# A hybrid decoder step on one core: the second half of the third block's step table put into a new order

## The reference, cut to what matters

```python
qp, fp, ip, gp = _split(jnp.einsum('bld,de->ble', h, w_in), C_SPLITS)
f = lower_bound + (1.0 - lower_bound) * jax.nn.sigmoid(fp)
q, k, log_f, v = silu(qp), 1.0 - f, log(f), ip          # each in 8 heads
...
A = cumsum(log_f)                                        # in _hgrn2
s = einsum('bhtk,bhtsk->bhts', q, exp(A_t - A_s) * k)    # causal
o = q exp(A) S + s v;   S_new = exp(A_end) S + k exp(A_end - A) v
...
o = _head_norm(o, hg_gn, False) * silu(gp)
return einsum('ble,ed->bld', o, w_out), S_new
```

## Time and profile before

| | |
|---|---|
| median of 3 runs | 1481.58 us (1480.04 to 1482.13) |
| profiled execution, own time | 1482.85 us |
| its span, first to last instruction | 1481.0 us |
| TensorE busy | 1455.0 us, 98% of the span |
| VectorE, ScalarE busy | 78%, 63% |
| mean granted TensorE clock | 0.994 |

### The profile page before, as it was taken

The page is one execution under the profiler, slowest core; times in us unless marked ns, Lnnn a source line. Parts: engine busy times, 40 slices in busy tenths (PEclk is TensorE's granted clock), DMA queues, the critical chain, the costliest instruction groups (busy, mean ns, idle before and its releaser), DMA issues.

```text
span 1481.0 us, 23131 instructions
## 1 busy us (share of the span) xinstructions
PE 1455.0 (98%) x8514; PEld 1288.9 (87%) x8514; DVE 1148.0 (78%) x1283; ACT 936.2 (63%) x983; POOL 82.4 (6%) x97
## 2 busy tenths in 40 slices
PE   9999999999999989999999999999999999999997
PEld 8889889999999989888888888888888888888885
DVE  5766687554556697776888988989889888898997
ACT  5354755334334675363877878778787787877875
POOL 1023100000001000120300000000000000000011
PEclk9999999999999999999999999999999999999999
DMA  8578636996456523542999999999999999999994
GB/s 233 143 144 144 126 101 186 309 297 186 122 143 193 167 86 105 154 128 75 408 408 409 410 365 393 366 401 391 357 392 364 401 387 364 393 376 385 394 344 163
DMA packets 213733, 404.06 MB, mean 273 GB/s; under 512 B 13487, under 2 KB 130507, under 8 KB 213534
## 3 DMA queue, kind: packets, MB, share of 16 engines
q1 hardware_dynamic: 203120, 373.62, 72.2%
q0 software_dynamic: 6320, 22.21, 5.0%
q10 hardware_dynamic: 4222, 7.26, 1.3%
HBM read 372.76 MB, written 30.28 MB: 272 GB/s over the span
## 4 chain that ended last, share of the span: by engine, by line
PE 89%; DVE 6%; ACT 2%; issue 1%; DMA 1%; POOL 1%; SPq 0%; DVEq 0%; ACTq 0%; POOLq 0%
PE bank L536 26%; PE bank L538 26%; PE bank L537 26%; PE bank L1234 1%; PE bank L830 1%; PE bank L1048 1%; POOL expert_rows L2796 1%; DVE dense_lo L1982 1%; PE bank L793 1%; DMA ring<-in_w_in_ab 1%; PE bank L763 1%; DVE w_lo L2494 1%; PE bank L704 1%; ACT dense_hi L1462 1%; DMA expert_rows<-arena,IDX 0%
## 5 line engine op out<-in xcount | busy, mean ns | idle before, releaser
L2494 DVE TENSOR_TENSOR w_lo<-arena,w_hi 128x2048 fp32r<-128x2048 f32 (+1 forms) x280 | 596.7, 2166 | 76.3 <-ACT w_hi L1823 75.5
L1823 ACT ACTIVATE w_hi<-arena 128x2048 fp32r<-128x2048 f32 (+1 forms) x280 | 501.8, 1820 | 116.0 <-PE bank L538 105.2
L536 PE MATMUL bank<-w_hi,xg_hi 128*128 128x512 f32 x704 | 275.6, 391 | 0.5 <-DVE w_lo L2494 0.3
L538 PE MATMUL bank<-w_hi,xg_lo 128*128 128x512 f32 x704 | 274.1, 389 | 0.0
L537 PE MATMUL bank<-w_lo,xg_hi 128*128 128x512 f32 x704 | 274.0, 389 | 0.0
L1982 DVE TENSOR_TENSOR dense_lo<-ring,dense_hi 128x2048 fp32r<-128x2048 f32 (+1 forms) x77 | 165.6, 2150 | 127.6 <-ACT dense_hi L1462 127.6
L1462 ACT ACTIVATE dense_hi<-ring 128x2048 fp32r<-128x2048 f32 (+1 forms) x78 | 140.5, 1802 | 136.0 <-PE bank L538 110.5
L536 PEld LDWEIGHTS bank<-w_hi,xg_hi 128*128 128x128 f32 x704 | 132.2, 188 | 30.8 <-issue 3.1
L538 PEld LDWEIGHTS bank<-w_hi,xg_lo 128*128 128x128 f32 x704 | 132.1, 188 | 27.6
L537 PEld LDWEIGHTS bank<-w_lo,xg_hi 128*128 128x128 f32 x704 | 132.2, 188 | 26.9
L536 PE MATMUL bank<-h_hi,dense_hi 128*128 128x320 f32 x448 | 143.2, 320 | 3.3 <-DVE h_lo_a L2052 1.8
(11 more groups left out here) (474 smaller groups left out, 2333.0 us busy)
## 6 DMA issues: line engine op xcount, KB each, us to landing
arena<-in_w_moe_down SPq DMA_DIRECT2D x176, 512.0 KB, 6.8
arena<-in_w_moe_gate SPq DMA_DIRECT2D x128, 512.0 KB, 7.7
arena<-in_w_moe_up SPq DMA_DIRECT2D x128, 512.0 KB, 7.4
arena<-in_w_moe_gate SPq DMA_DIRECT2D x64, 384.0 KB, 4.2
arena<-in_w_moe_up SPq DMA_DIRECT2D x64, 384.0 KB, 5.2
ring<-in_w_in_ab SPq DMA_DIRECT2D x32, 512.0 KB, 8.7
ring<-in_w_in_c SPq DMA_DIRECT2D x32, 512.0 KB, 4.6
expert_rows<-ZERO SPq DMA_DIRECT2D x12, 1024.0 KB, 7.7
```

Source lines behind the costliest of these rows:

```text
L536: mm(out, left[0], right[0], start=start, stop=False)
L538: return mm(out, left[1], right[0], start=False, stop=stop)
L1823: fn(WH[SLOT_OF[p]][:, 0:unit_size(p)], STAGE[:, s, 0:unit_size(p)], ACT.Copy).then_inc(S("unit_hi"), 1)
L2494: v.tensor_tensor(WL[w][:, 0:n], STAGE[:, s, 0:n], WH[w][:, 0:n].bitcast(F32), ALU.subtract).then_inc(S("unit_split"), 1)
```

## The change

Six of the table's nine rows are replaced by five; the first three rows and the first nine steps of the fourth (`xend0` to `thin0`) stay. Two rows of before, two of after, and the edits of code:

```diff
-    lb2 db3 state0 turn1 v7 xb3 lb3 sq0 v8 thin2 wh pb3 out1 wl v9 turn2 db4 out2 thin3 sq1 db5 xb4 lb4 state1 v10 state2
-    pb4 db6 xb5 g0 lb5 turn3 sq2 xb6 wh v11 pb5 out3 wh wl pb6 sq3 lb6 wl g1 db7 xb7 g2 pb7 g3 lb7 end1 state3
...
+    xb3 lb3 v5 wh pb3 db4 lb4 xb4 v6 pb4 db5 state0 turn1 xb5 lb5 sq0 v7 thin2 pb5 db6 wl out1 xb6 lb6 v8 wh sq1 turn2 pb6 db7
+    out2 thin3 state1 xb7 lb7 v9 wl pb7 end1 lb8 xend1 v10 state2 sq2 turn3 v11 wh kend1 out3 g0 wl sq3 state3 turn4 thin4 turn5 thin5
...
@@ ScalarE, step silug
-                    if u == 2:
-                        nc.scalar.preload_act_table_set("sqrt_and_others")
@@ ScalarE, step h
+                    if u == KD - 1:
+                        nc.scalar.preload_act_table_set("sqrt_and_others")
@@ VectorE, step mixc
+                    if u == HEADS[1][0]:
+                        after_empty(dve, ("sp", 1, KD - 1))
```

More of the change, by code:

```diff
@@ L78 @@
     q4 sig1 pa5 forget4 la5 q5 forget5 xa6 la6 wh forget6 forget7 pa6 ln1 da7 scan1 xa7 q6 q7 wl la7 end0 silu1 xb0 pa7 pb0
-    xend0 kend0 v0 v1 wh db1 lb0 turn0 thin0 wh xb1 wl lb1 v2 la8 v3 db2 pb1 thin1 v4 wl wh xb2 wl out0 v5 v6 pb2
-    lb2 db3 state0 turn1 v7 xb3 lb3 sq0 v8 thin2 wh pb3 out1 wl v9 turn2 db4 out2 thin3 sq1 db5 xb4 lb4 state1 v10 state2
-    pb4 db6 xb5 g0 lb5 turn3 sq2 xb6 wh v11 pb5 out3 wh wl pb6 sq3 lb6 wl g1 db7 xb7 g2 pb7 g3 lb7 end1 state3
-    xend1 wh g4 lb8 kend1 wl g5 turn4 thin4 turn5 thin5 silug0 out4 wh sq4 gate0 wl g6 along out5 sq5 gate1 thin6 state4 varc0 rootc0
-    turn6 gate2 gate3 state5 turn7 g7 along out6 sq6 silug1 silug2 mixc0 mixc1 mixc2 mixc3 state6 thin7 h0 h1 h2 h3 gate4
-    gate5 mixc4 mixc5 out7 sq7 gate6 h4 h5 varc1 rootc1 gate7 state7 wh wl mixc6 mixc7 h6 h7
+    xend0 kend0 v0 v1 wh db1 lb0 turn0 thin0 xb1 wl lb1 v2 wh pb1 la8 v3 db2 thin1 xb2 wl lb2 v4 out0 pb2 db3
+    xb3 lb3 v5 wh pb3 db4 lb4 xb4 v6 pb4 db5 state0 turn1 xb5 lb5 sq0 v7 thin2 pb5 db6 wl out1 xb6 lb6 v8 wh sq1 turn2 pb6 db7
+    out2 thin3 state1 xb7 lb7 v9 wl pb7 end1 lb8 xend1 v10 state2 sq2 turn3 v11 wh kend1 out3 g0 wl sq3 state3 turn4 thin4 turn5 thin5
+    g1 wh out4 sq4 state4 wl g2 along out5 sq5 thin6 turn6 g3 wh state5 silug0 gate0 gate1 wl out6 sq6 turn7 g4 gate2 gate3 varc0 rootc0 state6 thin7 g5 wh
+    mixc0 mixc1 mixc2 mixc3 wl g6 along out7 sq7 h0 h1 h2 h3 silug1 gate4 gate5 g7 varc1 rootc1 silug2 mixc4 mixc5 h4 h5 state7 gate6 gate7 mixc6 mixc7 wh h6 h7 wl
 """.split()]
```

## The result

Twelve runs of the changed kernel have a median of 1483.41 us (1481.42 to 1486.16), twelve of the kernel before 1481.32 (1479.91 to 1484.16): ratio 1.0017, 95% interval 1.0010 to 1.0024. The forecast was 1483.4. A second set (first experiment) gave 1484.22 against 1480.61, 1.0023 (1.0014 to 1.0032). By the means the changed kernel is 2.0 us slower in the first set and 3.1 us in the second, each against the kernel before beside it; the sum had said 1.8.

The account below looks back on a forecast made before the run. TensorE, busy 1455.0 of 1481.0 us, was taken as the bound. 5.4 us gone against 5.5 of new waits and 1.7 for the clock gave +1.8 us, a median of 1483.4 us, range 1479.0 to 1485.2.

Parts of the forecast that it names:

- the sum: Whole kernel: 5.4 us gone against 5.5 of new waits and 1.7 for the clock, +1.8 us.
- What is removed: TensorE's waits at lb6, low parts and head 7's squares, 3.7 us, plus 1.7 for half clock: 5.4 us gone.
- the forecast's own case: The waits change places and the clock falls once, behind the wait at lb8: 1483.4 us, chance 0.43.
- new wait 4: Output product's second unit: TensorE waits for its low part, 1.0 us (0.5 to 1.2).
- New wait 1: States of head 1: TensorE waits for ScalarE to empty bank 0 of head 2's turned keys, 1.2 us.
- New wait 2: At lb8: TensorE waits for VectorE's chain, 7.1 us against its own 4.54, so 2.5 us (2.1 to 2.8).
- place 2: The place at lb8 where New wait 2 was expected, 2.5 us.
- New wait 3: At lb6: GpSimd's store and spread fall on pb5, adding 1.6 us; TensorE waits 0.8 us (0 to 1.1).
- The clock: Half clock was taken to follow New wait 2, costing 1.7 us (bounds 0 and 1.7).
- no fall: Rival: the same new waits without half clock, +0.1 us, 1481.7 us; chance 0.27.
- a second fall: Rival: half clock also follows New wait 1 or New wait 3, +3.5 us, 1485.1 us; chance 0.17.
- The levels fit: Rival: new waits 1 to 3 stay away, only new wait 4 remains; 4.4 us won, 1477.2 us; chance 0.13.

Follow-up runs that it names:

- first experiment: The changed kernel run once more without an edit, listed as after_again: median 1484.22 us, ratio 1.0023 to the kernel before.
- keys_first: Changed kernel with a unit's high part moved behind head 2's turned keys on ScalarE: 1483.45 us, ratio 1.0011 to the kernel before.
- after_again: The changed kernel once more, no edit: 1484.22 us, ratio 1.0023 to the kernel before.
- lb8_only: Changed kernel with keys_first, scale_early and store_spread_late together, leaving only the wait at lb8: 1479.42 us, ratio 0.9991 to the kernel before.
- store_spread_late: Changed kernel with GpSimd's store of head 0's states and its spread both held until pb5 is done: 1483.36 us, ratio 1.0020 to the kernel before.
- spread_first: Changed kernel with GpSimd's spread for head 1 put ahead of its store of head 0's states: 1483.08 us, ratio 1.0021 to the kernel before.
- after: The changed kernel itself, first set of runs: 1483.41 us, ratio 1.0017 to the kernel before.
- scale_early: Changed kernel with TensorE's scales of heads 6 and 7 made two heads earlier in the output product: 1482.16 us, ratio 1.0010 to the kernel before.
- spread_late: Changed kernel with only GpSimd's spread for head 1 held until pb5 is done: 1482.60 us, ratio 1.0015 to the kernel before.
- low_behind: Changed kernel with VectorE's low part of a unit moved behind pb7 and the end's differences: 1480.62 us, ratio 1.0000 to the kernel before.
- all_mended: Changed kernel with keys first, low part behind, scales early, store and spread late: 1476.29 us, ratio 0.9969 to the kernel before.
- four_mends_spread_first: As all_mended, but with GpSimd's spread ahead of the store in place of the two late ones: 1476.52 us, ratio 0.9975 to the kernel before.

## Why the prediction was right

**What is removed.** The waits at the old `lb6` and for head 7's squares are gone, as the sum had it. Of the 1.2 for low parts 0.36 is still there, for head 6; it is counted under new wait 4. Half clock behind a wait is not gone but moved, as the forecast's own case said.

**New wait 1**: forecast 1.2, measured 1.21 in both profiles; keys_first shows the unit's high part on ScalarE as its cause.

**New wait 2**: forecast 2.5, measured 2.36 in after_again, 2.4 in keys_first, lb8_only, store_spread_late and spread_first. Where the clock fell ahead of it, it is 0.9 (after), 1.1 (scale_early) and 0.3 (spread_late, 6.8 us at half clock): TensorE, slowed, comes to it later. low_behind shows the low part as its cause. (The products that stood behind head 1's states before, `pb4`, are three levels ahead of `pb7`, not four as said with place 2.)

**New wait 3**: forecast 0.8, measured 1.09. The amount of the hold was right, 1.63 (2.58 against 0.95). Its cause was wrong in part: the store by itself takes nothing, the spread by itself 0.85, and the other 0.78 come only where the spread stands right behind the store. The Trainium skill, SBUF — State Buffer, section "Who interferes with whom", had inferred that descriptor writing does not block a VectorE instruction with two SBUF inputs: spread_late agrees, with 0.95 us beside it. The most that the prediction worked out from that page, the spread's 1.06, holds where the spread starts by itself (0.85); behind the store it was 1.63. In the trace VectorE's first product began at 586.04, the spread's record at 586.74; that a spread already queued behind the store holds VectorE from before its record begins is the reading that fits, and it was not tried by itself.

**New wait 4**: forecast 1.0, all of it for the unit's low part; measured 0.36 for head 6's low part, which the prediction had put at nothing, and 0.69 for the unit, 1.05 in all. TensorE waits for the same late chain in two places. scale_early shows that TensorE's own scale, queued behind five heads, set it.

**The clock.** The forecast (a fall behind wait 2) is what after_again, lb8_only, store_spread_late and spread_first show, four of the five profiles in which `lb8` waits its full 2.4 us; in keys_first, the fifth, none came in the block. In after, scale_early and spread_late the fall came 7 to 9 us earlier than in after_again, 1 to 2 us behind the wait at head 1's states; it stands ahead of `lb8`, so that wait can't be its cause. Four other profiles with the same 1.2 us at head 1 had no fall there. Where `lb8` hardly waits (low_behind, all_mended, four_mends_spread_first) none of the three had half clock between 580 and 690 us. The two profiles of the changed kernel have one fall each in the block, against the rivals "no fall" and "a second fall"; the price was paid in one of them and hidden by wait 2 in the other. What decides between the two places is not shown: the same waits were followed by a fall in one execution and not in another. The Trainium skill, TensorE: Matmul & The Clock Gate, section "What's actually happening", says that the gate does not start anew with a kernel; that fits a place which moves from execution to execution; that it is the reason, no run here shows.

**The sum.** Waits: 5.7 new less 3.7 gone is 2.0 where `lb8` waits in full; the forecast had 5.5 less 3.7, 1.8. By the means the changed kernel was 2.0 us slower in the first set and 3.1 in the second. In the second the mean granted clocks are 0.9967 before (31 runs) and 0.9959 after (12), 0.0008 of 1480 us or some 1.1 us, an estimate from clocks given to three digits; with the 2.0 it makes 3.1. I had taken fall for fall as equal; that is the term that was short there. So the block came out as summed, but that the median of the first set meets the forecast to 0.01 us is luck: the second set's is 0.8 higher, and in the first set's own profile the block lost only 0.3 us and late weights more than 5. "The levels fit" was wrong: the waits from TensorE's own last step came as counted.

## What to carry to other kernels

When an order is changed by hand, count for each step that TensorE waits for both sides from the last event that they share: here that gave three of four new waits to 0.3 us in the first profile (one of them split over two places, and one with its cause half wrong), and the fourth to 0.2 where the clock stayed up ahead of it. Then look in the same count for what can stand behind the awaited work: a unit's low or high part that nobody needs yet, or a scale queued behind products, was enough in three of four places, and the mends together were worth 7 to 8 us where the change itself had given 2 to 3 away. A wait that comes and goes from one profile to the next together with half clock ahead of it is one cost, not two.

## What was not expected of the hardware

GpSimd and VectorE can hold each other, and which of them waits is not settled by who was at work first. In spread_late VectorE was at work as the spread began: the spread took 4.69 us instead of 1.06 and VectorE's differences kept their 0.96. In spread_first VectorE was at work too, and it was VectorE that lost 0.85 while the spread took 1.04. With the store right ahead of the spread VectorE lost 1.63 in the changed kernel, and nothing in store_spread_late, where it was in the middle of its products and the spread took 3.55.

In one profile of eleven of the changed kernel and its variants (the first) loads of the last expert's down weights, issued as ever, landed late: the last of them 18.6 us after its issue, against 11.5 in the kernel before. TensorE then waited 3.47 us, and half clock followed. What held those loads was not found.
